# Two transformer blocks on one Trainium2 core: the second block's attention heads in pairs on array halves, one PSUM bank a 256-token block, and weight splits ahead of emptying

## The reference

```python
# layer 0, mixer a: 16 heads of 64, three groups g that see keys at strides 1, 4, 16
h = x @ w_in                                # 10 x 1024 columns: q, k, v of each g, and z
for g in range(3):
    q, k = rope(q_g), rope(k_g)
    s_g = where(mask_g, q @ k.T / 8, -inf)  # per head, 256 x 256, causal
o = softmax over all three groups' keys at once, times v
y = (o * silu(z)) @ w_out
# layer 1, mixer b: 16 query heads, 2 key/value heads, window of 128, a sink logit per head
s = where(band, rope(q) @ rope(k).T / 8, -inf); m = max(s, sink)
o = exp(s - m) @ v / (sum exp(s - m) + exp(sink - m))
y = (o * silu(z)) @ w_out
# after each mixer
v = layer_norm(ALPHA * x + y)
x = v + sigmoid(v @ w_gate) * (p @ w_proj)
```

## Time and profile before

| what | value |
|---|---|
| median of three runs | 1861.16 us (1853.01 to 1865.01) |
| the profiled execution's own time | 1855.55 us |
| its span | 1853.3 us |
| PE busy | 1648.4 us, 89% of the span |
| DVE busy | 1062.3 us, 57% |
| ACT busy | 929.2 us, 50% |

### The profile page before, as it was taken

The page is one execution under the profiler, slowest core; times in us unless marked ns, Lnnn a source line. Parts: engine busy times, 40 slices in busy tenths (PEclk is TensorE's granted clock), DMA queues, the critical chain, the costliest instruction groups (busy, mean ns, idle before and its releaser), DMA issues.

```text
span 1853.3 us, 26621 instructions
## 1 busy us (share of the span) xinstructions
PE 1648.4 (89%) x10291; PEld 1388.9 (75%) x10291; DVE 1062.3 (57%) x1967; ACT 929.2 (50%) x1668; POOL 105.4 (6%) x114
## 2 busy tenths in 40 slices
PE   6899888869999999779997699989999999798787
PEld 3577566637888888547665599989899998797676
DVE  1563546675343434575636776678566674576655
ACT  4353545434232313245545455558677785477635
POOL 3100023020000000020012100000000000000000
PEclk8799978888999999889987899999999999998889
DMA  8422445302323333212455256555442432342221
GB/s 291 136 68 69 159 159 180 112 28 85 120 91 92 97 107 97 70 49 67 130 161 186 91 162 201 187 178 181 144 159 92 160 121 85 114 137 76 84 69 69
DMA packets 221567, 225.45 MB, mean 122 GB/s; under 512 B 6155, under 2 KB 219985, under 8 KB 221393
## 3 DMA queue, kind: packets, MB, share of 16 engines
q1 hardware_dynamic: 220736, 223.63, 37.6%
q0 software_dynamic: 704, 0.12, 0.0%
HBM read 222.68 MB, written 1.05 MB: 121 GB/s over the span
## 4 chain that ended last, share of the span: by engine, by line
PE 71%; ACT 12%; DVE 11%; issue 3%; DMA 2%; POOL 0%; SPq 0%; DVEq 0%; ACTq 0%; POOLq 0%
PE bank L795 18%; PE bank L796 17%; PE bank L797 17%; ACT whi L1245 2%; ACT AP L1599 2%; PE bank L820 1%; ACT SH L1360 1%; PE bank L1023 1%; DVE XT L1999 1%; PE bank L866 1%; PE bank L864 1%; PE bank L865 1%; DMA raw<-in_w_mod_dram 1%; DVE AP L2221 1%; DVE wlo L1729 1%
## 5 line engine op out<-in xcount | busy, mean ns | idle before, releaser
L1729 DVE TENSOR_TENSOR wlo<-raw,whi 128x1024 fp32r<-128x1024 f32 (+3 forms) x322 | 389.5, 1210 | 326.6 <-ACT whi L1245 322.7
L1245 ACT ACTIVATE whi<-raw 128x1024 fp32r<-128x1024 f32 (+3 forms) x322 | 337.3, 1047 | 361.4 <-PE bank L797 329.1
L795 PE MATMUL bank<-HH,whi 128*128 128x512 f32 (+3 forms) x656 | 254.5, 388 | 34.6 <-DVE HL L1751 29.5
L796 PE MATMUL bank<-HL,whi 128*128 128x512 f32 (+3 forms) x656 | 250.5, 382 | 0.0
L797 PE MATMUL bank<-HH,wlo 128*128 128x512 f32 (+3 forms) x656 | 250.3, 382 | 0.0
L795 PE MATMUL bank<-HA,whi 128*128 128x256 f32 x576 | 166.8, 290 | 14.8 <-DVE LA L1751 7.4
L795 PEld LDWEIGHTS bank<-HH,whi 128*128 128x128 f32 (+2 forms) x656 | 123.3, 188 | 68.9 <-issue 23.6
L796 PE MATMUL bank<-LA,whi 128*128 128x256 f32 x576 | 163.7, 284 | 0.0
L797 PE MATMUL bank<-HA,wlo 128*128 128x256 f32 x576 | 163.6, 284 | 0.0
L797 PEld LDWEIGHTS bank<-HH,wlo 128*128 128x128 f32 (+2 forms) x656 | 123.7, 188 | 26.8 <-issue 1.0
L796 PEld LDWEIGHTS bank<-HL,whi 128*128 128x128 f32 (+2 forms) x656 | 123.9, 189 | 25.5 <-issue 1.5
(11 more groups left out here) (342 smaller groups left out, 3494.0 us busy)
## 6 DMA issues: line engine op xcount, KB each, us to landing
raw<-in_w_ff_dram SPq DMA_DIRECT2D x64, 1024.0 KB, 5.3
raw<-in_w_mod_dram SPq DMA_DIRECT2D x48, 1024.0 KB, 5.2
raw<-in_a_w_in_dram SPq DMA_DIRECT2D x40, 1024.0 KB, 5.0
raw<-in_w_in_dram SPq DMA_DIRECT2D x16, 1024.0 KB, 5.2
raw<-in_b_w_in_dram SPq DMA_DIRECT2D x9, 1024.0 KB, 5.2
raw<-in_w_out_dram SPq DMA_DIRECT2D x8, 1024.0 KB, 5.1
raw<-in_ple_w_gate_dram SPq DMA_DIRECT2D x8, 1024.0 KB, 5.2
raw<-in_a_w_out_dram SPq DMA_DIRECT2D x4, 1024.0 KB, 5.1
```

The lines of the kernel that those rows point to most:

```text
L795: nc.tensor.matmul(o, wh, xh, start=start, stop=False)
L796: nc.tensor.matmul(o, wh, xl, start=False, stop=False)
L1245: f(whi[h % HALF_SLOTS][:, 0:n], raw[u.id % RAW_SLOTS][:, (h % 2) * n:(h % 2) * n + n], ACT.Copy)\
L1729: v.tensor_tensor(wlo[h % HALF_SLOTS][:, 0:n], raw[u.id % RAW_SLOTS][:, (h % 2) * n:(h % 2) * n + n], whi[h % HALF_SLOTS][:, 0:n].bitcast( ...
```

## The change

**Packed units.** `Unit.packed` is true for units of two blocks of 128 on 256 tokens (not bkv). Both blocks go to one PSUM bank, columns 0 to 255 and 256 to 511, with the start flag on the first block's first matmul alone. So three units are in the three banks, and a signal is given once a unit. The emptying takes both blocks in one instruction: 4 rope copies of 32x512 and 3 DVE operations of 128x512 (the cosine and sine tables are read with a broadcast over the two blocks), one copy or silu of 128x512, and so on for the first block's layer 1, out2, proj and gate.

**Splits ahead.** `halves_ahead` counts both halves of u+2 for a packed unit. Both splits are called before the emptying on ACT and DVE.

**Pairs.** A step now takes two heads e=0, 1: rows 0 to 63 and 64 to 127 of one tile. Scores: first queries 0 to 127 (`att2_first`, banks 3 and 6), then the others (`att2_second`, banks 4, 5 and 6, 7), e=0 and e=1 in turn. P times V puts the heads on the two column halves (64 columns of V each, output partitions 64e to 64e+63 of bank 5). APT is twice as large. The scale is in `late`, the low part of y too, and y's high and low part follow each pair.

**Order.** Layer 0 has a table of slots by unit; layer 1 one `b_step` a unit.

```diff
@@ class Unit @@
+        self.packed = (blocks is not None and kind not in ("mod", "bkv") and [m for _, m in blocks] == [P, P]
+                       and all(b - a == SEQ for a, b in t))
@@ the list of steps @@
+    for p, at_units in enumerate(((10, 11, 13, 14), (14, 15, 17, 18), (20, 21, 23, 24), (24, 25, 27, 28),
+                                  (30, 31, 32, 33), (33, 34, 35, 36), (36, 37, 38, 40), (39, 40, 41, 42))):
+        for kind, n in zip(("att2_first", "att2_second", "att2_turn", "att2_pv"), at_units):
+            a_slots.setdefault(n, []).append((kind, (0, p)))
...
+    def b_step():
...
+        if p >= 2:
+            steps.append(("att2_pv", (1, p - 2)))
+        if 1 <= p <= PAIRS:
+            steps.append(("att2_turn", (1, p - 1)))
+        if p < PAIRS:
+            steps.append(("att2_first", (1, p)))
+            steps.append(("att2_second", (1, p)))
...
+                    a_step(10 * hq + n)
                     fm(aw, 0, col, 256, two, kind, (i, hq, g), x, seq2)
-                    if hq > 0 and n < 4 or hq == 3 and n >= 7:
-                        att2_step()
...
-                   att2_step if n >= 1 else None)
-                if n >= 1:
-                    att2_step()
+                   b_step if n == 7 else None)
+                b_step()
@@ how far splits have to be @@
-        u.halves_ahead = u.halves_next + sum(v.id == u.id + 2 for v in split_units)
+        u.halves_ahead = u.halves_next + (2 if u.packed else 1) * sum(v.id == u.id + 2 for v in split_units)
@@ PE: a packed unit's bank @@
+                        if u.packed and bi == 0:
+                            both = next_bank((u.id, 0), *block_readers(u, 0), *block_readers(u, 1))
+                            bank_of[(u.id, 1)] = bank_of[(u.id, 0)]
+                            open_[0], open_[1] = both[:, 0:SEQ], both[:, SEQ:T]
@@ PE: scores @@
+                for e in (0, 1):
+                    r = slice(64 * e, 64 * e + 64)
+                    k_ = AK[buf][r, g, blk, :] if i == 0 else AK[0][r, 0, p // 4, :]
+                    ins = nc.tensor.matmul(dst[e][:, g * n:(g + 1) * n], q[r, g, blk, part * P:part * P + P], k_[:, 0:n],
+                                           start=True, stop=True)
@@ PE: P times V @@
-                nc.tensor.matmul(b[:, 0:SEQ], v(g, 0), APT[:, g * SEQ:(g + 1) * SEQ], start=g == 0, stop=False)
+                for e in (0, 1):
+                    nc.tensor.matmul(b[64 * e:64 * e + 64, 0:SEQ], v(g, 0, e), att_pt(ip, e)[:, g * SEQ:(g + 1) * SEQ], start=g == 0, stop=False)
@@ ACT: rope copies @@
+                    ins = f(SH[sh_turn[0] % 2][32 * q:32 * q + 32, 0:n, :], b[32 * o:32 * o + 32, 0:n, :], ACT.Copy)
@@ DVE: rope @@
+                cos, sin = (bc(rope[:, w:w + 1, :], [P, m, SEQ]) for w in (0, 1))
+                sh, rr = SH[n % 2][:, 0:m, :], RR[n % 2][:, 0:m, :]
+                dve.wait_ge(s_sh2, s_sh2.at(key))
+                v.tensor_tensor(rr, b, cos, ALU.mult).then_inc(*s_cos2.tick(key))
+                v.tensor_tensor(sh, sh, sin, ALU.mult).then_inc(*s_sin2.tick(n))
```

More of the change, by code:

```diff
@@ L857, in unit @@
                         pe.wait_ge(ready, ready.at(u.x[1:] + (k,)))
-                        first, final = k == 0, k == KC - 1
+                        first, final = k == 0 and not (u.packed and bi == 1), k == KC - 1
                         if u.kind == "av":
@@ L1095, in att2_turn @@
-        def att2_turn(ih, batches):
-            i, h = ih
+            if i == 0 and part == 0:
+                dst = [acquire(3 + 3 * e, (s_mx2, (ip, part, e))) for e in (0, 1)]
+            elif i == 0:
+                for b in range(4, 8):
+                    acquire(b, (s_mx2, (ip, part, b // 6)))
+                dst = [wide, wide_odd]
+            elif part == 0:
+                dst = [acquire(3 + 3 * e, (s_mx2, (ip, 1, e))) for e in (0, 1)]
+            else:
+                dst = [banks[3][:, P:], banks[6][:, P:]]
```

574 lines of the change are left out of this document (319 added, 255 removed).

## The result

The changed kernel takes 1846.85 us (median of 11 runs, 1840.82 to 1852.05) where the one before takes 1859.6 (median of 11 runs beside it, 1853.01 to 1874.8). The ratio is 0.9932, 95% interval 0.991 to 0.9955: faster by 0.7%, 13 us. The forecast was 1809.5 with a range of 1782 to 1840, so the sign is right, the size is a quarter of it, and the time lies outside the range. The profiled execution has a span of 1841.3 us, 12.0 under that of before.

The account below looks back on a forecast made before the run. PE was taken to bound layer 0, with PE waiting on DVE and ACT in layer 1. From the profiled 1855.55 us, minus 25 (layer 0), 17 (layer 1) and 4 (the rest) gave 1809.5, range 1782 to 1840.

Parts of the forecast that it names:

- PE's work a pair: Layer 0: P times V, scores and transposes of two heads take 6.6 us on PE, bounds 6.3 and 10.3.
- rival 1: The two heads' halves don't overlap and a pair keeps its 10.3 us; about 1840, chance 8%.
- rival 3: Slower: DVE's rope with a broadcast table costs up to 1.64 us an operation instead of 0.69; 1868.5, chance 5%.
- The tail: End of layer 0, 24.9 us before: 16.8 worked out, 8 less.
- 210 + 17 = 227 instead of 248: Layer 0's window: 210 us of PE's work without a wait plus 17 of new waits, 21 less than before.
- the prediction's own sign: Wrong if layer 0 from first head to out2 isn't shorter by 15 us at least, or layer 1 by 8.
- 30 units are 163 us of the 248.: Layer 0: weight units on PE at 5.44 us each, from the distance of two units' splits on ACT.
- The new waits: Layer 0: PE waits 13 us at three turns of hq 3, 4.4 each, and 4 at the other four turns.
- minus 17: Layer 1: periods of 12.6 us with aq and 10.2 with az make it 20 shorter, 3 given back.
- minus 4: The rest: gains at gate, proj and the first block's output projection against losses at stage ends; bounds plus 5 and minus 11.
- The ends of stages: Where a stage ends with a packed unit, the last emptying comes later, at five or six ends: plus 7 us.
- Rival 2: ACT and DVE become the bound, with longer turn waits in layer 0 and longer layer 1 periods; about 1830, chance 12%.

Follow-up runs that it names:

- x1_lag: Changed kernel with layer 0's turns two units behind their scores, last pair apart; layer 0's heads take 251.2 us, 11.4 less than in the changed kernel.
- x7_border_late: Changed kernel with layer 1's units reordered, plus layer 1's ACT splits after the emptying, DVE's at the next unit's start; layer 1 99.3 us, 108.6 with reordering alone.
- x10: x1_lag's slots and x7_border_late's layer 1 together, plus bkv's value blocks in one bank and the last gate unit emptied at once before splits; bkv 8.7 us, not 16.2.
- x5_ahead1: Changed kernel with one half of the unit after next split ahead again, packing and pairs kept; layer 0's heads 12.1 us more, bkv 8.1 us instead of 16.4.
- x6: Changed kernel with packed banks and splits ahead in the second block alone, the first block's second layer emptied block by block; 1839.53 us.
- x11_all: x10 plus one half split ahead in ff1 and ff2 units of the first block's second layer; 1811.38 us, ratio 0.9742 to the kernel before.

## Why the prediction was wrong, by its steps

**Right.** The sign, and PE's work a pair: 6.42 us for the 6.6 taken, in the lower part of its bounds of 6.3 to 10.3; rival 1 falls. DVE's rope with its broadcast table takes 0.69 us, rival 3 falls:

```profile
L1944 DVE TENSOR_TENSOR RR<-bank,rope_sb 128x512 f32<-128x512 f32 x24 | 16.6, 691 | 17.6 <-ACT SH L1434 17.1
...
L1945 DVE TENSOR_TENSOR SH<-SH,rope_sb 128x512 f32<-128x512 f32 x24 | 16.4, 681 | 0.0
```

The rope copies of 32x512 take 2.39 us for four (2.1 taken, within 1.55 to 3.10). The tail is 6.6 shorter (8 forecast).

**Wrong, layer 0: "210 + 17 = 227 instead of 248", measured 249.** Shorter by 5.5 us with its tail and not by 15, layer 0 is wrong by the prediction's own sign. The 22 us that are missing lie in three terms of the sum.

1. "30 units are 163 us of the 248." By the starts in PE's row, the weight matmuls of that window take 175.2 us, 12 more. They took 174.4 before too, beside 68.9 of heads and 4.8 of waits. The window holds half a unit more than 30 (3 us), 711 of its 1465 matmuls run at 117.8 ns (3 us), and the rest is spread over starts behind other forms of the array and borders of units. This term was set at nothing, and the slip could have been seen without a run: put to the kernel before, the same sum (163 of units, 69 of heads, 5 of waits) gives 237 and not the 248 that the earlier trace rows show.
2. The new waits: 17 us in the sum, 25 by the starts in the row, 24.4 of them named in the waits view. The turns of the last quarter wait 5.2, 6.1 and 2.6, near the 4.4 each, and the other four 2.9 for the 4 taken. What was missed is 4.5 us of P times V waiting for ACT's copies and 3.1 of pair 6's scores waiting for the rope of the unit just ahead, the same kind of wait as in layer 1.
3. The transposes at the lower clock after the long waits, 5 us, stood nowhere.

Together 25 us. Against them the pairs' own work in the window is 3.4 us under the 47.1 of the sum, mostly since one P times V falls behind its end. The mechanism of the last quarter was in the text; its place in the sum was too small. x1_lag shows it as cause, 11.4 us of it in the table of slots alone.

**Wrong, layer 1: "minus 17", measured 9.1.** The step that failed is the list of what a period holds: it goes through ACT and DVE only. With an aq unit, PE's scores stand in the loop too, since they wait for its rope and the maxima wait for them: 1.6 us and a handover. From scores to scores, the four az periods take 9.6 to 11.1 us, near the 10.2 forecast, and the first of them is 10.2 (1668.99 to 1679.22). The three aq periods were forecast at 12.6 and take 14.4 (1679.22 to 1693.65), 15.3 and 15.7. The first has just those 1.8 us more. In the second the maxima start 0.9 us later after the scores than in the first, behind the low part of y on DVE, which waits for ACT. So from the first exponentials to the last pass 85.7 us in place of 78.6. The end behind them takes 8.3 in place of 5.4, the start 19.4 in place of 18.0, and 3 had been given back. That the loop over ACT and DVE was the right thing to add up, x7_border_late supports.

**Wrong, the rest: "minus 4", measured plus 2.7.** The gains at gate and proj came: out2 to gate takes 5.5 and 6.3 us less in the two layers (9 were forecast together). bkv wasn't in the text at all. It takes all three banks and the whole of x, both of which now come from one packed gate unit emptied in one piece behind two splits: 3.6 us of wait and 4.8 at a lower clock, 8.4 in all. Its wait and the slow stretch went with x10, and with x5_ahead1. The ends of stages were priced at 7; the last ff2 unit with its norm alone costs 3.2, by x5 and x6 both.

**Rival 2 was nearest in its mechanism.** It said that ACT and DVE become the bound and gave 1830 with a chance of 12%; measured is 17 us more, so its size was too small as well. The Trainium skill, TensorEngine Tiling (Array Packing), section PSUM Bottleneck, says that tiling speeds up TensorE but not PSUM evacuation; this case agrees in kind: 31 us of PE's work gone in layer 0, 5.5 us of time, though the largest wait there is for DVE's scale, which is no evacuation. I had weighed it as one possible mishap, although spoke for it. The splits ahead, that I had counted as a cost alone, save 12 us in layer 0 once the banks are packed (x5_ahead1), waits and clock together; there the sum had the wrong sign, and was better for it by luck.

## What to carry to other kernels

When an engine's work shrinks between two steps of a fixed latency chain, add up the chain (here scores, rope or emptying, maxima, exponentials, scale) against what the engine has to do meanwhile: the saving counts only down to that length. Write down each loop with every engine that it passes, in the order of their queues, and ask of each split, copy or load whether it stands inside; moves of splits, turns and units alone gave 35 us between the changed kernel and x11_all (with one bank less for bkv), where pairs, packing and splits ahead had given 13. Put the sum for the new kernel to the old one first: if it doesn't give what the old one measures, the difference is no gain. A unit that takes all buffers of a rotation, or all of its input, shows the whole latency of the step ahead of it, and packing lengthens that latency.

## What the runs showed of the hardware that was not expected

Fp32 matmuls on two halves of the array overlap fully when they alternate: one pair's P times V, twelve records of 256 tokens and twelve of 128, takes 2.10 us, and one head's had taken 1.96. They overlap even when three of one head stand ahead of three of the other, with a lag of 0.49 us (2.58 us in all) and with records starting out of the order of the program (L1193 at 1349.22, L1190 at 1349.28). Matmuls of 256 columns run at one of two paces, 113.3 or 117.8 ns from start to start, at the same granted clock of 1.00; 50 us hold 444 or 427. In the ff stage the pace changes only at a gap, and moved the stage by up to 6.6 us between kernels with the same matmuls; elsewhere it also changes from one unit to the next without one (before, at 1311.1, 47 matmuls at the slower pace follow 143 at the faster). And after a wait the granted clock may fall for much longer than the wait: 17.0 us at 0.72 after 3.6 us, 13.9 us at 0.63 after 1.3, and not at all after 0.4 or, before, after 2.8. Much of what stages differ by is this: in layer 0's heads the granted clock is 0.93 in x5_ahead1, 0.97 in the changed kernel and 0.99 in x11_all.
